# Weights of two neighbouring k tiles stored column by column in turn, so that a matmul loads its 128 columns with a step of two words

## What is computed

```
h = rms_norm(x, norm_mix)
u = h @ w_in                       # 1024 x 5248: attention, RWKV and merge columns
o_nsa, o_rwkv = nsa(u), rwkv7(u)   # small matmuls, softmax, a scan
y = gates[0] * (o_nsa @ proj_nsa) + gates[1] * (o_rwkv @ proj_rwkv)
x = x + y @ w_out
x = x + conv_ffn(rms_norm(x, norm_ffn), ffn_up, ffn_conv, ffn_down)
# second block: ffn, hybrid mixer (attention and mLSTM), ffn
x = x + 0.5 * rms_norm(swiglu(rms_norm(x, g1), w_gate, w_up, w_down), g2)
x = x + rms_norm(hybrid_mixer(rms_norm(x, g3), w_in_2, ..., w_out_2), g4)
x = x + 0.5 * rms_norm(swiglu(rms_norm(x, g5), w_gate2, w_up2, w_down2), g6)
```

## Time and profile before

| | |
|---|---|
| time, median of 3 runs | 2433.51 us (2431.32 to 2433.78) |
| the profiled execution: its own time, and its span | 2431.45 us, 2429.6 us |
| granted TensorE clock, mean over the span | 0.992 of 2.4 GHz |
| PE busy | 2378.4 us, 98% of the span |
| PEld busy | 1953.2 us, 80% |
| DVE, ACT, POOL busy | 1065.1, 935.4, 1034.3 us (44%, 38%, 43%) |
| DMA | 204.21 MB, mean 84 GB/s |

### The profile page before, as it was taken

The page is one execution under the profiler, slowest core; times in us unless marked ns, Lnnn a source line. Parts: engine busy times, 40 slices in busy tenths (PEclk is TensorE's granted clock), DMA queues, the critical chain, the costliest instruction groups (busy, mean ns, idle before and its releaser), DMA issues.

```text
span 2429.6 us, 38821 instructions
## 1 busy us (share of the span) xinstructions
PE 2378.4 (98%) x13906; PEld 1953.2 (80%) x13906; DVE 1065.1 (44%) x1843; ACT 935.4 (38%) x1278; POOL 1034.3 (43%) x754
## 2 busy tenths in 40 slices
PE   8999998899999999999999999999999999999999
PEld 6878777778888888888888877888888888888887
DVE  4456475455555522222222855763333448222212
ACT  3345432243555533444423322224444624444322
POOL 3322230035454555455555633443333355555554
PEclk9999999999999999999999999999999999999999
DMA  5211110023232233222233322221222232222332
GB/s 159 70 44 44 61 62 3 3 92 98 87 96 99 99 104 104 95 95 95 95 106 109 101 70 70 86 80 62 87 78 78 70 104 69 95 95 97 102 104 95
DMA packets 60732, 204.21 MB, mean 84 GB/s; under 512 B 10940, under 2 KB 11708, under 8 KB 60380
## 3 DMA queue, kind: packets, MB, share of 16 engines
q1 hardware_dynamic: 55152, 196.45, 24.7%
q10 hardware_dynamic: 5488, 6.44, 0.9%
HBM read 200.76 MB, written 2.10 MB: 83 GB/s over the span
## 4 chain that ended last, share of the span: by engine, by line
PE 87%; DVE 9%; issue 2%; ACT 1%; POOL 1%; DMA 0%; SPq 0%; DVEq 0%; ACTq 0%
PE psum L403 85%; DVE rope_t L2540 2%; DVE qk_st L2539 2%; POOL x L388 1%; PE psum L650 1%; DVE rope_t L2532 1%; DVE qk_st L2542 1%; PE psum L1090 0%; DVE inv L2157 0%; DVE tmp L2458 0%; ACT dd L1437 0%; DVE a_t L2098 0%; PE psum L772 0%; DVE zm L1799 0%; DVE h_lo L1833 0%
## 5 line engine op out<-in xcount | busy, mean ns | idle before, releaser
L376 POOL TENSOR_TENSOR w_lo<-raw,w_hi 128x512 fp32r<-128x512 f32 x732 | 1006.3, 1396 | 1377.3 <-ACT w_hi L1243 1377.3
L403 PE MATMUL psum<-h_hi,w_hi 128*128 128x512 f32 x2128 | 852.8, 401 | 13.7 <-DVE h_lo L1833 10.6
L403 PE MATMUL psum<-h_lo,w_hi 128*128 128x512 f32 x2128 | 835.4, 393 | 0.0
L1243 ACT ACTIVATE w_hi<-raw 128x1024 fp32r<-128x1024 f32 x366 | 386.1, 1055 | 684.7 <-PE psum L403 669.0
L403 PE MATMUL psum<-h_hi,w_lo 128*128 128x512 f32 x2128 | 535.4, 390 | 0.0
L403 PEld LDWEIGHTS psum<-h_hi,w_hi 128*128 128x128 f32 x2128 | 403.5, 190 | 112.4 <-issue 26.6
L403 PEld LDWEIGHTS psum<-h_lo,w_hi 128*128 128x128 f32 x2128 | 403.5, 190 | 83.6 <-issue 3.2
L403 PEld LDWEIGHTS psum<-h_hi,w_lo 128*128 128x128 f32 x2128 | 399.0, 188 | 83.9 <-issue 0.5
L1799 DVE TENSOR_TENSOR tmp<-psum,rst 128x512 f32<-128x512 f32 x100 | 69.1, 691 | 322.5 <-PE psum L403 322.2
L403 PE MATMUL psum<-hid_hi,w_hi 128*128 128x512 f32 x528 | 205.4, 389 | 0.0
L403 PE MATMUL psum<-hid_lo,w_hi 128*128 128x512 f32 x528 | 205.4, 389 | 0.0
(11 more groups left out here) (427 smaller groups left out, 2605.1 us busy)
## 6 DMA issues: line engine op xcount, KB each, us to landing
raw<-in_w SPq DMA_DIRECT2D x366, 512.0 KB, 3.3
x<-in_x SPq DMA_DIRECT2D x4, 512.0 KB, 6.3
x<-in_x ACTq DMA_DIRECT2D x1, 2048.0 KB, 7.9
out_y<-x SPq DMA_DIRECT2D x8, 256.0 KB, 2.3
mask<-in_mask ACTq DMA_DIRECT2D x1, 1536.0 KB
tmp<-in_cmp_w ACTq DMA_DIRECT2D x2, 512.0 KB, 5.7
masks<-in_masks ACTq DMA_DIRECT2D x1, 768.0 KB, 4.3
lora<-in_lora ACTq DMA_DIRECT2D x1, 512.0 KB, 3.2
```

The source lines that it names most:

```text
L376: pool.tensor_tensor(w_lo[:, g.slot, part], raw[:, g.slot, part], w_hi[:, g.slot, part].bitcast(F32), ALU.subtract).then_inc(sem("lo_ready ...
L403: return pe.matmul(out, lhsT, rhs, start=start, stop=stop)
L1243: act.activation(w_hi[:, g.slot], raw[:, g.slot], ACT.Copy).then_inc(sem("hi_ready"), 1)
```

## The change

The words of `w_hi` and `w_lo` are stored in another order. The 1024 words of a slot are four groups of 256; in a group, the columns of k tile 2q and of k tile 2q + 1 stand in turn: column 0 of the one, column 0 of the other, column 1 of the one, and so on. `raw` and the units in HBM stay as they are. ACT reads `raw` in order and writes `w_hi` with a step of two words. POOL reads `raw` in order, reads `w_hi` and writes `w_lo` with a step of two words; a half is still 512 words, now as two groups of 256. A matmul's weights are 128 words with a step of two. The built program has the same instructions in the same order on every engine, with the same semaphores; the sizes and the values computed are the same. In the changed kernel the lines behind the three new functions stand 12 or 13 lines further down.

```
+        def by_column(t, slot):
+
+            return t[:, slot].rearrange("p (q c a) -> p q a c", a=2, c=128)
+
+        def of_raw(slot):
+
+            return raw[:, slot].rearrange("p (q a c) -> p q a c", a=2, c=128)
+
+        def weights(t, slot, k):
+
+            return by_column(t, slot)[:, k // 2, k % 2]
+
...
                 for n in range(2):
-                    part = slice(512 * n, 512 * n + 512)
-                    pool.tensor_tensor(w_lo[:, g.slot, part], raw[:, g.slot, part], w_hi[:, g.slot, part].bitcast(F32),
+                    part = slice(2 * n, 2 * n + 2)
+                    pool.tensor_tensor(by_column(w_lo, g.slot)[:, part], of_raw(g.slot)[:, part],
+                                       by_column(w_hi, g.slot)[:, part].bitcast(F32),
                                        ALU.subtract).then_inc(sem("lo_ready"), 1)
...
             def mm_hi(out, slot, k, hi, lo, start):
-                a = w_hi[:, slot, tok(k)]
+                a = weights(w_hi, slot, k)
                 mm(out, a, hi, start, False)
                 mm(out, a, lo, False, False)
...
             def mm_lo(out, slot, k, hi, stop):
-                return mm(out, w_lo[:, slot, tok(k)], hi, False, stop)
+                return mm(out, weights(w_lo, slot, k), hi, False, stop)
...
-                act.activation(w_hi[:, g.slot], raw[:, g.slot], ACT.Copy).then_inc(sem("hi_ready"), 1)
+                act.activation(by_column(w_hi, g.slot), of_raw(g.slot), ACT.Copy).then_inc(sem("hi_ready"), 1)
```

## The result

The changed kernel takes 2482.43 us (median of 4 runs, 2482.09 to 2483.2) against 2433.65 us (4 runs, 2431.32 to 2435.98): 1.0201 times the time before, interval 1.0183 to 1.0219. It is slower by 49 us; the forecast was 79 us faster. The profiled execution has a span of 2481.4 us, 51.8 more than before.

What follows compares the result with a forecast made beforehand. TensorE's packed matmuls, pitch 226.7 ns times 8640, were taken as the bound; 54 + 18 + 2 + 3.5 + 1 us made 79 saved, 2431.45 - 79 = 2352, the runs' median 2 us above: 2354 us, range 2338 to 2494.

Steps and rivals of the forecast that it cites:

- My reading, which no row proves: TensorE's split-weight matmuls: weight loads touching the same memory part as the moving operand cause the 13.4 ns surplus.
- the term of 9.7 x 8640 = 84 us: All 8640 split-weight matmuls: pitch falls from 226.7 to 217 ns, saving 84 us before the share reaching the end.
- the sign for the load as the limit: TensorE's weight loads: the bound on them is wrong if they start more than 217 ns apart with nothing else late.
- rival 1: Matmul stream: nothing changes, the surplus belongs to full rate and the moving operand's addresses; 2433 us, chance 0.16.
- Float32 as a price: Matmul pitch: taken as 217 ns from the float32 stream, where a load runs beside it and costs nearly nothing.
- The proj row: Proj, operand tiles 513 words apart: 234 ns a matmul, surplus 21, between the pitch bounds of 217 and 240.
- The load's own speed: TensorE's weight loads: a step of two words is as fast as dense, next load possible after 110 ns.
- How much reaches the end: All stages: 79 of 84 us reach the end; mix gives nine tenths, rwkv and merge half.
- ACT, POOL and what is late next: ACT's copy up to 1.6 us, POOL's half 2.0 us, both hidden, cost nothing; nothing new becomes the bound.
- Rival 3: Weight loads: the stream loses a moment per stretch of memory a load comes to; 2542 or 2492 us, chance 0.20.
- its lower price: Matmul pitch under slower loads: proj's 234 ns, 59 us more, 2492 us; half of the 0.20 chance.
- a toll for each stretch of memory: Matmul stream: a load spanning 1024 bytes in place of 512 costs twice the surplus, 240 ns, 109 us more.

Runs made afterwards that it cites:

- e9: Kernel before, with the unit matmuls reading only the upper two bytes of each word as bfloat16, weights and moving operand both: 2410.43 us, one run.
- e1: Changed kernel with the step of two words only in TensorE's loads, ACT and POOL writing in order: 2483.09 us, 1.0212 times the kernel before.
- e2: Changed kernel with the step of two words only in ACT and POOL, TensorE's loads dense: 2433.95 us, 1.0 times the kernel before.
- e3: Kernel before, dense writes, with loads in steps of 8 and 4 words for `w_hi` and 4 for `w_lo`: 2545.43 us, one run.

## Why the prediction was wrong

**The step that failed** is "My reading, which no row proves": that the 13.4 ns of surplus are collisions between load and stream, which a load at the stream's own speed would avoid. With it went the term of 9.7 x 8640 = 84 us, which came out with the other sign: 6.67 ns more, 57.6 us by all 8640. None of the signs that the prediction gave was made for this: the pitch was neither 217 nor still 226.7, and loads starting more than 217 ns apart, the sign for the load as the limit, only came with the longer pitch, since strided loads can start 0.11 us apart. What the runs show in its place:
- No kernel ran these matmuls with a surplus below 11.7 ns (two bytes); dense loads gave 13.3 at 512 columns and mostly at 384, and 16 to 18 between. No change of the loads took it away: not a quarter of the columns (18 ns), not a single word read 128 times in every third load, not another place. That much of rival 1 was right. No run streamed without any loads, so whose it is at bottom stays open.
- What the loads decide is what comes on top: 0 for dense loads on multiples of 256 bytes against 512 columns, 2.2 ns at 64 bytes off, 5 for 32 columns, 6.7 for the step of two, 9 to 15 for steps of four and eight words (where the load's own pace may have a part). The kernel before already had the best of these; no arrangement tried at full size and type beat it.
- What in the strided load holds the stream up, and why it costs 6.7 ns where all matmuls have 512 columns and 0 to 2.9 elsewhere, is not shown. That two streams of the same operands and shapes stand at 226.7 and 225.0 (e9) and that full matmuls lose 226.7 among shorter ones speak for the pattern that a stream settles into, and not for a fixed price of a load; no run tests this by itself.

The Trainium skill (TensorE: Matmul & The Clock Gate, Part 2) has separate read ports for the moving operand and the weights, so that a load takes no read bandwidth from the running matmul. The trace doesn't agree that a load leaves this stream alone: the step in the loads alone (e1) moved its pitch from 226.7 to 233.3. Whether bandwidth is what it takes, no run here shows. At 384 columns the trace agrees: 173.3 ns over long stretches with either load.

**Float32 as a price.** I took 217 ns, the float32 stream's, as the value for loads that get out of the way. It was the wrong neighbour: it has two column times for each column, and what its loads would cost a stream at full rate it can't show. The proj row, which I had as the upper part of the range, 234, was the near one. There the operand's place is awkward, here the load's, and both ended 20 ns above 213.3; with both at once, in proj after the change, it is not more.

**The load's own speed** was right: two strided loads can start 0.11 us apart, as dense ones can. The Trainium skill (SBUF — State Buffer, Door 1, the box on lines) asks for two hits in a line of 16 bytes. The trace agrees: 193 ns against 188 at two words, where a line is hit twice, and 310 at four, where it is hit once. But a load that is as fast as before was no reason for the stream to be.

**How much reaches the end**: 0.94 was assumed, 0.92 came in the profiled execution and 0.87 by the medians. Mix passed on 9.6 of 13.6 us, 0.71, where I had nine tenths; the up and down stages all. For rwkv and merge, 2.9 of 4.8 where I had half, one trace decides nothing: this stage is 3.4 us longer than before in the trace of e2 too, whose pitch is that of before.

**ACT, POOL and what is late next** were right: 1132 ns of the 1600 allowed, a median of 1312 ns of the 2000, nothing new in PE's waits, and e2 at 1.0.

**Rival 3** at its lower price, 234 ns and 2492 us, came closest to the 2482, and the range of 2338 to 2494 holds the result only because that price, with a chance of 0.10, was taken into it: luck, by its mechanism. Its place was right, the loads, but a toll for each stretch of memory would give 247 or more at a step of four (it was 236 for `w_lo`, e3), would hold at 384 columns (it was 0), and would fall with 32 columns (it rose). What spoke against it on record, proj's 21 ns under equal loads, was sound; it spoke against the mechanism and not against the price.

## What to carry to other kernels

In a packed stream of matmuls the distance between starts is the first number to take, and a surplus in it isn't to be credited to weight loads until a kernel that changes only the loads has moved it. Dense weights on multiples of 256 bytes against full 512 columns were the best arrangement found here; another order of the same words cost 3% of the pitch though neither the length of the loads nor any wait shows it. What such an order costs is to be measured in the stream itself: the same step cost 6.7 ns there and 0 to 2.9 in streams of other lengths. Of the two rows that were to stand for the new pitch, the one of the same type and rate, proj, was the nearer here; the float32 row misled.

## What was not expected of the hardware

- A load of 32 columns lasts 109 ns instead of 188 and makes the stream slower: 231.6 ns against 226.7.
- 504 columns take as long as 512 when the loads are dense: 226.8 and 226.7 ns. A full matmul among shorter ones takes 229 to 232.
- 64 bytes of shift between weights and activations cost 0.53% of the kernel's time (0.34 to 0.73), 256 bytes nothing that can be measured.
- Pitches settle into short patterns that repeat, such as 226, 229 and 232 ns, in kernels whose matmuls all have the same shape.
- A load with a step of four words takes 310 ns in place of 188, and eight in a row cost the stream only 9 ns each.
